# A one-core chain of four transformer layers in fp32: how the kernel passes from one matrix product to the next

## The chip, the cores and the metric

The kernel runs on one core of one Trainium2 chip. Its time is the device time of one execution in microseconds. Before the change it took 2042.35 us, the median of three runs (2042.11 to 2044.91).

## What is computed

A residual stream x of 256 positions by 1024 features passes through two blocks of two layers each.

```python
# first block, l = 0, 1
h = h + mixer_l(rms_norm(h, mix_norm_g[l]))             # l=0: attention || gated linear attention; l=1: RG-LRU
h = h + conv_ffn(rms_norm(h, ffn_norm_g[l]), ...)       # x @ w_up, causal conv, u*gelu(g), @ w_down
x = rms_norm(h, final_norm_g)
# second block, l = 0, 1
x = x + 0.5 * rms_norm(swiglu(rms_norm(x, ffn1_pre[l]), ...), ffn1_post[l])
x = x + rms_norm(hybrid_mixer(rms_norm(x, mix_pre[l]), ...), mix_post[l])
x = x + 0.5 * rms_norm(swiglu(rms_norm(x, ffn2_pre[l]), ...), ffn2_post[l])

def rms_norm(x, g): return x * rsqrt(mean(x * x, -1) + 1e-6) * g
def swiglu(h, w_gate_up, w_down): g, u = split(h @ w_gate_up, 2); return (silu(g) * u) @ w_down
```

The inner widths are 3072 (first block) and 2816 (second). All data are fp32 and all weights are read once.

## The kernel before

**Layout.** Features lie on the 128 partitions and the 256 positions on the free axis, so x is 8 tiles of 128x256. A weight matrix comes from memory as chunks of 16 blocks of 128x128 (1 MB). A chunk usually holds 8 blocks along the inner dimension for each of two output tiles. There are 313 chunks.

**A product in three.** Each fp32 operand is split in two fp32r parts: ScalarE rounds a raw chunk (`w_raw`) to `w_hi` (`round_chunk`, L222), VectorE takes the rest `w_lo` (`rest_chunk`, L230), and in the same way `x_split` (L315 hi, L320 lo) and `h_split` hold the two parts of an activation. TensorE then does three matmuls of 128x128 by 128x256 per block: hi·hi (L246), hi·lo (L248) and lo·hi (L250), 48 for a chunk, into one PSUM bank that holds the chunk's two output tiles.

**Rings.** `w_raw`, `w_hi`, `w_lo` and the PSUM banks are rings of `RING = 3`. When chunk n is multiplied, ScalarE rounds chunk n+3 (`refill_hi`) and VectorE makes the rest of chunk n+2 (`refill_lo`). SyncE fetches raw chunk n once the rest of chunk n-3 is done. TensorE waits before a chunk for its `w_lo` and for `pair_taken`; this starts at 2, so that it runs at most two chunks ahead of VectorE's evictions although there are three banks.

**Order.** Every engine has its instruction stream written out in program order, with semaphores; there is no scheduler. A pass through the program is, in phases: ev_in, attention, ev_out, up0, down0, od_xr, od_gate, od_ax, od_out, up1, down1, then twice upA, downA, bg, pool_in, cv, gates, conv_out, pool, pool_out, w_o, upB, downB. The chunks within a phase mostly stand in register loops of three, and the two layers of the second block are one outer loop on each engine.

**Norms.** `rms_norm` is applied after the product: a phase that begins with a norm (`pre_pe`) multiplies x times the gain, and its results are scaled by 1/rms when they are taken out of PSUM (`take_scaled`, L264). The 1/rms vector is made on the way. Squares are summed on ScalarE and VectorE, TensorE sums over partitions (`mean_pe`, L285, in the middle of the second chunk), ScalarE takes the root (`rms_act`, L291), VectorE the reciprocal and two diagonal matrices (`rinv_dve`, L296, L299), TensorE spreads them to all partitions (`rinv_pe`, L305) and ScalarE copies (`rinv_act`, L311).

**The two kinds of transition.** Where a residual is added at once (ev_out, down0, od_out), `out_dve` adds the product to x (L458) pair by pair and the next phase's splits follow. Where a norm stands after the product (down1, downA, w_o, downB), nothing of the next phase can start before the norm is known: `out_pe`, `out_act`, `out_dve`, then `mean_pe`, `rms_act`, `rinv_dve`, `rinv_pe`, then `post_dve`, `post_act` and `post_pool`, which apply the norm (L377), add it to x (L383 on VectorE for pairs 0 and 2, L399 on GpSimd for pairs 1 and 3), and split x for the next phase. I call this a post transition; there are seven, the last one ends the kernel.

## Time and profile before

| | |
|---|---|
| median of 3 runs | 2042.35 us |
| the profiled execution | 2043.53 us |
| its span, first to last instruction | 2041.7 us |
| TensorE matmul busy | 1899.5 us (93%) |
| VectorE busy | 1372.9 us (67%) |
| ScalarE busy | 942.4 us (46%) |
| granted TensorE clock, mean | 0.96 of full |

The profile gives for each engine when an instruction ran and what ended the idle time before it. Matmuls overlap, so the duration of one (285 ns) is not the time that it adds: the distance between two starts is.

### The profile page before, as it was taken

The page shows a single profiled execution, that of the slowest core. Times are in us where ns is not written, and L with a number is a line of the kernel's source. Part 1 is how long each engine was busy: PE and PEld are TensorE (multiplying, and loading weights), DVE is VectorE, ACT ScalarE, POOL GpSimd, SP SyncE. Part 2 cuts the span into 40 slices and gives each one's busy share as a digit, 9 for nine tenths or more (in the row PEclk, how much of TensorE's full clock was granted, in tenths as well). Part 3 has the DMA queues.
Part 4 walks back from the last instruction along what each step waited for, and adds up shares of the span by engine and source line. Part 5 has one row for each costly group of instructions (what it writes and reads, how often), then busy time and mean ns, then how long its engine had stood idle before and what let it go on. Part 6 is the DMA issues. An engine that isn't in the chain of part 4 may idle for free.

```text
span 2041.7 us, 38654 instructions
## 1 busy us (share of the span) xinstructions
PE 1899.5 (93%) x15258; PEld 1864.6 (91%) x15258; DVE 1372.9 (67%) x1651; ACT 942.4 (46%) x1103; POOL 145.6 (7%) x134
## 2 busy tenths in 40 slices
PE   7969999996999989998999999998999899989996
PEld 7948999996999989997999889998999899989996
DVE  4796898477899456655775666656654686675656
ACT  4443665455666444443354444434443335344444
POOL 0000222000122000000300000000000120000000
PEclk9968999997999989998999999998999899989998
DMA  6312455542455435453444435543554345444453
GB/s 257 131 42 104 169 178 180 183 165 98 171 185 182 179 134 185 179 194 140 168 180 172 169 141 183 188 185 128 182 206 186 124 166 185 166 144 166 184 207 123
DMA packets 46756, 337.27 MB, mean 165 GB/s; under 512 B 5184, under 2 KB 5568, under 8 KB 5952
## 3 DMA queue, kind: packets, MB, share of 16 engines
q1 hardware_dynamic: 46512, 335.34, 45.2%
q8 instruction: 71, 1.16, 0.2%
q0 software_dynamic: 144, 0.52, 0.1%
q14 instruction: 29, 0.24, 0.0%
HBM read 334.80 MB, written 1.05 MB: 164 GB/s over the span
## 4 chain that ended last, share of the span: by engine, by line
PE 60%; issue 29%; DVE 7%; POOL 2%; ACT 2%; DMA 0%; ACTq 0%; POOLq 0%; SPq 0%; DVEq 0%
PE psum L246 19%; PE psum L250 19%; PE psum L248 19%; DVE w_lo L230 1%; POOL scratch L1279 1%; DVE scratch L1126 1%; POOL x_resid L399 0%; DVE scratch L377 0%; DVE x_split L320 0%; POOL scratch L1276 0%; DVE scratch L1372 0%; PE psum L305 0%; DVE scratch L264 0%; DMA params<-par_in 0%; DVE scratch L1096 0%
## 5 line engine op out<-in xcount | busy, mean ns | idle before, releaser
L246 PE MATMUL psum<-x_split,w_hi 128*128 128x256 f32 x3272 | 939.3, 287 | 54.6 <-DVE x_split L320 26.2
L222 ACT ACTIVATE w_hi<-w_raw 128x2048 fp32r<-128x2048 f32 x316 | 604.9, 1915 | 813.8 <-PE psum L250 807.7
L248 PE MATMUL psum<-x_split,w_hi 128*128 128x256 f32 x3272 | 933.2, 285 | 0.0
L250 PE MATMUL psum<-x_split,w_lo 128*128 128x256 f32 x3272 | 933.0, 285 | 0.0
L230 DVE TENSOR_TENSOR w_lo<-w_raw,w_hi 128x2048 fp32r<-128x2048 f32 x315 | 722.2, 2294 | 55.8 <-ACT w_hi L222 55.8
L246 PEld LDWEIGHTS psum<-x_split,w_hi 128*128 128x128 f32 x3272 | 635.6, 194 | 66.3 <-issue 46.0
L248 PEld LDWEIGHTS psum<-x_split,w_hi 128*128 128x128 f32 x3272 | 636.0, 194 | 0.1
L250 PEld LDWEIGHTS psum<-x_split,w_lo 128*128 128x128 f32 x3272 | 635.6, 194 | 0.0
L246 PE MATMUL psum<-h_split,w_hi 128*128 128x256 f32 x1664 | 475.4, 286 | 25.8 <-DVE h_split L1252 18.4
L248 PE MATMUL psum<-h_split,w_hi 128*128 128x256 f32 x1664 | 473.4, 284 | 0.0
L250 PE MATMUL psum<-h_split,w_lo 128*128 128x256 f32 x1664 | 473.2, 284 | 0.0
L246 PEld LDWEIGHTS psum<-h_split,w_hi 128*128 128x128 f32 x1664 | 322.0, 193 | 29.0 <-issue 22.7
L264 DVE TENSOR_TENSOR scratch<-psum,inv_rms 128x512 f32<-128x512 f32 (+1 forms) x205 | 140.8, 689 | 306.3 <-PE psum L250 278.5
L248 PEld LDWEIGHTS psum<-h_split,w_hi 128*128 128x128 f32 x1664 | 322.2, 194 | 0.0
L250 PEld LDWEIGHTS psum<-h_split,w_lo 128*128 128x128 f32 x1664 | 322.0, 194 | 0.0
L560 DVE SCALAR_TENSOR_TENSOR scratch<-scratch,params 128x255 f32<-128x255 f32 x192 | 123.2, 702 | 8.1 <-ACT scratch L506 8.0
L399 POOL TENSOR_TENSOR x_resid<-x_resid,scratch 128x512 f32<-128x512 f32 x12 | 17.4, 1450 | 1228.3 <-DVE scratch L377 1228.3
L460 DVE COPY scratch<-psum 128x512 f32<-128x512 f32 x24 | 16.6, 692 | 111.8 <-PE psum L250 111.8
L498 ACT ACTIVATE h_split<-scratch 128x256 f32 (+1 forms) x136 | 55.1, 405 | 20.2 <-POOL scratch L608 12.7
L614 POOL TENSOR_TENSOR h_split<-scratch,h_split 128x256 f32 (+1 forms) x48 | 44.4, 926 | 165.9 <-ACT h_split L498 165.9
L458 DVE TENSOR_TENSOR x_resid<-psum,x_resid 128x512 f32<-128x512 f32 x16 | 11.1, 692 | 66.8 <-PE psum L250 66.8
L492 ACT ACTIVATE scratch<-scratch 128x256 f32<-128x256 f32 x136 | 54.8, 403 | 0.3
(178 smaller groups left out, 944.9 us busy)
## 6 DMA issues: line engine op xcount, KB each, us to landing
w_raw<-stream_in SPq DMA_DIRECT2D x316, 1024.0 KB, 4.8
x_resid<-x_in SPq DMA_DIRECT2D x1, 1024.0 KB, 6.9
y_out<-x_resid SPq DMA_DIRECT2D x1, 1024.0 KB, 3.9
scratch<-mask_in SPq DMA_DIRECT2D x1, 768.0 KB, 12.8
scratch<-ev_in SPq DMA_DIRECT2D x1, 512.0 KB, 11.4
scratch<-inv_in POOLq DMA_DIRECT2D x1, 512.0 KB, 4.0
params<-par_in SPq DMA_DIRECT2D x1, 247.0 KB, 7.1
matrices<-mat_in SPq DMA_DIRECT2D x1, 192.0 KB, 8.8
```

What stands on the lines that cost most here:

```text
L222: act.activation(w_hi[:, slot, :], raw[:, slot, :], ACT.Copy).then_inc(hi_ready, 1)
L230: dve.tensor_tensor(w_lo[:, slot, :], raw[:, slot, :], w_hi[:, slot, :].bitcast(F32), ALU.subtract).then_inc(lo_ready, 1)
L246: pe.matmul(dst, w_hi[:, c.slot, b:b + P], src[:, k0 + k, 0, :], start=first and k == 0 and m == 0, stop=False)
L248: pe.matmul(dst, w_hi[:, c.slot, b:b + P], src[:, k0 + k, 1, :], start=False, stop=False)
L250: done = pe.matmul(dst, w_lo[:, c.slot, b:b + P], src[:, k0 + k, 0, :], start=False, stop=last and k == nk - 1 and m == tiles - 1)
L264: dve.tensor_tensor(dst, bank(c.slot, tiles), rinv[:, :].unsqueeze(1).to_broadcast([P, tiles, T]), ALU.mult).then_inc(pair_taken, 1)
L492: act.activation(S1(GEL + s), S1((ACC + 2 * s + 1) if conv else (PRE + 2 * s)), func)\
L498: act.activation(hs[:, bass.ds(c.n - prev, 1), 0, :], S(HID + s), ACT.Copy)\
L560: dve.scalar_tensor_tensor(out=scr[:, ACC + 2 * s + t, d:T], in0=scr[:, PRE + 2 * s + t, 0:T - d], scalar=conv[0][:, bass.ds(((c.n - prev) ...
L614: pool.tensor_tensor(hs[:, bass.ds(c.n - prev, 1), 1, :], S(HID + s), hs[:, bass.ds(c.n - prev, 1), 0, :].bitcast(F32), ALU.subtract)\
L1126: ins = dve.tensor_tensor(qd(t)[o:o + 32, h * P:(h + 1) * P].rearrange("p (m n) -> p m n", n=n), E[o:o + 32, :, 1, :], Q[o:o + 32, :, 1, : ...
L1279: pool.tensor_tensor(S(DIFF, 2), S(DIFF, 2), pair, ALU.subtract).then_inc(*pool_diff.one())
```

## The change

- **Rings.** `RING` is 4 for `w_hi` and `w_lo`, `w_raw` keeps 3 buffers (`RAWS`). PSUM has `BANKS = 4` for chunk pairs, and `pair_taken` starts at 4. ScalarE now rounds chunk n+4 after chunk n, VectorE makes the rest of n+3.
- **First two chunks together.** `alternating` runs the first two chunks of a norm phase, and of the phases with one chunk for each output pair (ev_out, od_out, conv_out, pool_out, w_o), side by side in two banks: first all that needs the hi part of the activation, tile by tile, then all that needs the lo part.
- **Last tile apart.** In the last group of an output phase, the last chunk is multiplied output tile by output tile (`tile_by_tile`), tile 7 in a bank of its own (`SPLIT`), so that tile 6 is taken out while tile 7 is multiplied.
- **Sum of squares.** At a post transition TensorE sums the squares of tiles 0 to 5, 6 and 7 in three steps; the squares of tile 7 are read from PSUM. In a norm phase the mean stands in the third chunk after its fourth of eight steps, and the spreading after its seventh.
- **1/rms.** The diagonal matrices are gone: TensorE multiplies the reciprocal, broadcast as the stationary matrix, by the identity (two 128x128 matmuls for one of 128x256).
- **`post_dve`** does all residual additions on VectorE (GpSimd does none), in the groups 0, 1, 2-3, 4-5, 6-7, and all lo splits after them. The refills for the last chunk go behind it.
- **Straight code.** All register loops but SyncE's are written out, the outer loop too; the per-layer copy of the parameters goes. Three padding chunks are no longer fetched and split.
- **End and start.** The result leaves in four transfers, each after its pair of tiles; the last post transition makes no splits. At the start raw chunk 2 is fetched after the constants, and the spreading for ev_in comes as before after chunk 1.

The diff, cut to its core (`self.bank`, `self.buf` and renamed calls are left out):

```diff
-RING = 3
+RING = 4
+RAWS = 3
+BANKS = 4
+SPLIT, AXBANKS = 5, (4, 5, 7)
...
         def refill_lo(dve, c):
-            rest_chunk(dve, (c.slot + 2) % RING, c.number + 2)
+            rest_chunk(dve, c.number + RING - 1)
...
+        def alternating(pe, first, second, src, nk, hi, lo, k0=0):
+            both = (first, second)
+            for c in both:
+                pe.wait_ge(pair_taken, c.event + 1)
+                pe.wait_ge(lo_ready, c.number + 1)
+            for k in range(nk):
+                pe.wait_ge(*hi(k0 + k))
+                for c in both:
+                    for m in range(2):
+                        b = (k * 2 + m) * P
+                        for w in (w_hi, w_lo):
+                            pe.matmul(tile(c.bank, m), w[:, c.slot, b:b + P], src[:, k0 + k, 0, :],
+                                      start=k == 0 and m == 0 and w is w_hi, stop=False)
+            for k in range(nk):
+                pe.wait_ge(*lo(k0 + k))
+                for c in both:
+                    for m in range(2):
+                        b = (k * 2 + m) * P
+                        done = pe.matmul(tile(c.bank, m), w_hi[:, c.slot, b:b + P], src[:, k0 + k, 1, :],
+                                         start=False, stop=k == nk - 1 and m == 1)
+                    if k == nk - 1:
+                        done.then_inc(chunk_done, 1)
...
-                ins = dve.tensor_scalar(diag[:, h, :], IDENT, small[:, 4 + h:5 + h], float(D),
-                                        ALU.mult, ALU.mult)
+                ins = pe.matmul(RINV[:, h * P:(h + 1) * P], small[:, 4 + h:5 + h].to_broadcast([P, P]), IDENT,
+                                start=h == 0, stop=h == 1)
...
+        def tile_by_tile(pe, c, both, src, k0, nk, first, ready, tr, post, l):
+            for m, dst in enumerate(both):
+                for k in range(nk):
+                    ...
+                    if post is not None and m == 1 and k == nk // 2:
+                        pe.wait_ge(*tr["acc"].count(2, l))
+                        sums_pe(pe, (sqacc[:, 0, :], sqacc[:, 1, :]), True, False)
+                done.then_inc(*(tr["tile6_done"].one() if m == 0 else (chunk_done, 1)))
+            if post is not None:
+                pe.wait_ge(*tr["sq6"].count(1, l))
+                sums_pe(pe, (sqb[:, 0, :],), False, False)
+                pe.wait_ge(*tr["sq7"].count(1, l))
+                sums_pe(pe, (sqb[:, 1, :],), False, True).then_inc(*post["stat"].one())
+                rinv_pe(pe, post, l)
...
+            for ks in ((0,), (1,), (2, 3), (4, 5), (6, 7)):
+                k, n = ks[0], len(ks)
+                for j in ks:
                     h = x[:, j, :] if final else S1(HB + j)
                     dve.scalar_tensor_tensor(out=h, in0=h, scalar=gain[:, j:j + 1], in1=RINV, ...)
+                if not final:
+                    dve.wait_ge(*tr["y"].count(k + n, l))
+                    dve.tensor_tensor(x[:, k:k + n, :], x[:, k:k + n, :], S(HB + k, n), ALU.add)
+            for k in range(KT):
+                split_lo(dve, nxt, ngain, k, next_layer)
...
+            refill_lo(dve, last)
...
-            for c in chunks(act, phase, n, l, peel=3):
-                at = c.n if isinstance(c.n, int) else n
+            for c in chunks(phase, n, l):
+                at = c.n
                 act.wait_ge(chunk_done, c.number + 1)
-                if at == 1:
-                    rinv_act(act, pre, l)
                 refill_hi(act, c)
                 if at == 0:
                     chunk0 = c
+                    continue
+                if at == 1:
                     rms_act(act, pre, l)
-                    continue
+                    rinv_act(act, pre, l)
...
+            for g in range(4):
+                sp.wait_ge(*post_x(PN["postB"], 2 * g + 1, LAYERS2 - 1, False))
+                sp.dma_start(out[:, 2 * g:2 * g + 2, :], x[:, 2 * g:2 * g + 2, :]).then_inc(out_landed, 16)
```

On VectorE, from the end of downA to the take-out of bg's first chunks, the program had these rows before (registers left out; L460 takes out the last pair, L472 adds its squares, L230 is a weight chunk's rest):

```order
L460 COPY scratch<-psum 128x512 [waits chunk_multiplied]
...
L472 TENSOR_TENSOR square_sum<-square_sum,squares 128x512 [waits downA_squared]
...
L230 TENSOR_TENSOR w_lo<-w_raw,w_hi 128x2048 [waits chunk_hi_ready]
...
L296 RECIPROCAL small<-small 128x2 [waits postA_stat]
...
L299 TENSOR_SCALAR inv_rms_diagonal<-matrices,small 128x128 [waits postA_stat]
L299 TENSOR_SCALAR inv_rms_diagonal<-matrices,small 128x128
...
L377 SCALAR_TENSOR_TENSOR scratch<-scratch,params_layer,psum 128x256 [waits postA_stat]
```

and has these now, down to the same take-out (L512 tiles 6 and 7, L394 the norm, L399 the residual, L338 the lo splits, L219 a weight chunk's rest, L280 the take-out):

```order
L512 COPY scratch<-psum 128x256 [waits downA_tile6_done]
L512 COPY scratch<-psum 128x256 [waits downA_sq7,chunk_multiplied]
L316 RECIPROCAL small<-small 128x2 [waits postA_stat]
L394 SCALAR_TENSOR_TENSOR scratch<-scratch,params,psum 128x256 [waits postA_stat]
L399 TENSOR_TENSOR x_resid<-x_resid,scratch 128x256 [waits postA_y_ready]
...
L338 SCALAR_TENSOR_TENSOR x_split<-x_resid,params,x_split 128x256 [waits normM_hi_ready] x8
L410 TENSOR_TENSOR square_sum<-scratch 128x512 [waits postA_squared]
L410 TENSOR_TENSOR square_sum<-square_sum,scratch 128x512 [waits postA_summed,postA_squared] x2
L219 TENSOR_TENSOR w_lo<-w_raw,w_hi 128x2048 [waits chunk_hi_ready] x3
L316 RECIPROCAL small<-small 128x2 [waits normM_stat]
L280 TENSOR_TENSOR scratch<-psum,inv_rms 128x512 [waits chunk_multiplied,normM_stat]
```

The weight rest and the diagonals are gone from between the squares and the norm; three rests stand together ahead of the next phase's reciprocal. On ScalarE the same stretch now reads (L495, L502 squares of tiles 6 and 7, L311 the root, L333 the hi splits, L210 a weight chunk rounded, L329 the copy of 1/rms):

```order
L495 ACTIVATE squares<-scratch 128x256 [waits downA_tile6_taken]
L502 ACTIVATE squares<-psum 128x256 [waits chunk_multiplied]
L311 ACTIVATE small<-psum,small 128x2 [waits postA_stat]
L333 ACTIVATE x_split<-x_resid,params 128x256 [waits postA_x_ready] x8
L382 ACTIVATE scratch<-x_resid 128x512 x4
L210 ACTIVATE w_hi<-w_raw 128x2048 [waits chunk_landed_2]
L210 ACTIVATE w_hi<-w_raw 128x2048 [waits chunk_landed_0,chunk_multiplied]
L210 ACTIVATE w_hi<-w_raw 128x2048 [waits chunk_landed_1,chunk_multiplied]
L311 ACTIVATE small<-psum,small 128x2 [waits normM_stat]
L329 ACTIVATE inv_rms<-psum 128x256 [waits normM_stat]
```

where before the root of the next norm stood behind two rounded chunks of that stretch (one after the last chunk, one after bg's first), and now behind three.

## Rows read from the trace of the kernel before

**Rows 1.** The page: span, and busy time of two engines.

```profile
span 2041.7 us, 38654 instructions
PE 1899.5 (93%) x15258; PEld 1864.6 (91%) x15258; DVE 1372.9 (67%) x1651; ACT 942.4 (46%) x1103; POOL 145.6 (7%) x134
```

**Rows 2.** Stretches: length, busy and (matmuls) by engine, granted clock, DMA share, GB/s.

```profile
30.00:50.00 20.00, 20.00 (x169) 20.00 (x168) 8.67 (x6) 5.75 (x3) 0.00 (x0) 1.00 0.49 172
230.00:330.00 100.00, 100.00 (x836) 100.00 (x835) 96.16 (x108) 60.37 (x86) 28.55 (x36) 1.00 0.52 186
940.00:945.00 5.00, 4.75 (x22) 4.45 (x21) 4.97 (x10) 1.81 (x4) 1.56 (x2) 0.50 0.01 3
1010.00:1100.00 90.00, 90.00 (x752) 90.00 (x751) 60.38 (x70) 42.24 (x48) 0.00 (x0) 1.00 0.50 181
```

**Rows 3.** Timeline of the post transition from downA to bg, by engine.

```profile
930.09 0.28 PE L250 MATMUL psum<-h_split,w_lo 128*128 128x256 f32 x1
930.40 0.69 DVE L460 COPY scratch<-psum 128x512 f32<-128x512 f32 x1 [5.84 <-PE psum L250]
931.13 0.63 ACT L443 ACTIVATE squares<-scratch 128x512 f32<-128x512 f32 x1 [3.04 <-DVE scratch L460]
932.40 2.29 DVE L230 TENSOR_TENSOR w_lo<-w_raw,w_hi 128x2048 fp32r<-128x2048 f32 x1
932.54 1.05 PE L285 MATMUL psum<-matrices,square_sum 128*128 128x1 f32 x8 [2.17 <-DVE square_sum L472]
933.63 0.26 ACT L291 ACTIVATE small<-psum,small 128x2 f32<-128x2 f32 x1 [1.87 <-PE psum L285]
934.60 0.16 DVE L296 RECIPROCAL small<-small 128x2 f32<-128x2 f32 x1
935.33 1.22 PE L305 MATMUL psum<-inv_rms_diagonal,matrices 128*128 128x256 f32 x2 [1.74 <-DVE inv_rms_diagonal L299]
936.59 0.87 DVE L377 SCALAR_TENSOR_TENSOR scratch<-scratch,params_layer,psum 128x256 f32<-128x256 f32 x2 [1.31 <-PE psum L305]
937.49 0.69 DVE L383 TENSOR_TENSOR x_resid<-x_resid,scratch 128x512 f32<-128x512 f32 x1
938.22 0.91 ACT L315 ACTIVATE x_split<-x_resid,params_layer 128x256 fp32r<-128x256 f32 x2 [2.53 <-DVE x_resid L383]
939.51 0.55 PE L246 MATMUL psum<-x_split,w_hi 128*128 128x256 f32 x1 [2.96 <-DVE x_split L320]
956.88 0.35 PE L246 MATMUL psum<-x_split,w_hi 128*128 128x256 f32 x1 [1.44 <-DVE scratch L264]
```

**Rows 4.** Other waits of TensorE in the timeline.

```profile
173.53 0.38 PE L246 MATMUL psum<-h_split,w_hi 128*128 128x256 f32 x1 [1.49 <-DVE h_split L1184]
431.76 0.36 PE L246 MATMUL psum<-x_split,w_hi 128*128 128x256 f32 x1 [1.77 <-issue]
493.00 0.58 PE L246 MATMUL psum<-h_split,w_hi 128*128 128x256 f32 x1 [1.40 <-DVE h_split L1252]
1006.28 0.38 PE L246 MATMUL psum<-x_split,w_hi 128*128 128x256 f32 x1 [3.07 <-DVE w_lo L230]
1115.68 0.38 PE L246 MATMUL psum<-h_split,w_hi 128*128 128x256 f32 x1 [1.09 <-DVE scratch L1372]
1384.58 0.58 PE L246 MATMUL psum<-x_split,w_hi 128*128 128x256 f32 x1 [5.39 <-issue]
```

**Rows 5.** The page: a weight chunk rounded and fetched.

```profile
L222 ACT ACTIVATE w_hi<-w_raw 128x2048 fp32r<-128x2048 f32 x316 | 604.9, 1915 | 813.8 <-PE psum L250 807.7
w_raw<-stream_in SPq DMA_DIRECT2D x316, 1024.0 KB, 4.8
```

**Rows 6.** Timeline at the end of the kernel, and the result's transfer.

```profile
2028.39 0.87 DVE L377 SCALAR_TENSOR_TENSOR scratch<-scratch,params_layer,psum 128x256 f32<-128x256 f32 x2 [1.31 <-PE psum L305]
2035.73 1.44 POOL L399 TENSOR_TENSOR x_resid<-x_resid,scratch 128x512 f32<-128x512 f32 x1 [3.44 <-DVE scratch L377]
2037.25 0.35 SPq L1420 DMA_DIRECT2D y_out<-x_resid  x1
```

More of the change, by code:

```diff
@@ L242, in multiply @@
                     pe.wait_ge(*ready(k0 + k))
[L243 removed]
+                for m, dst in enumerate(tiles_):
                     b = (blk0 + k * 2 + m) * P
[L245 to L251 removed]
@@ L252, in multiply @@
-                if midway is not None and k == nk // 2 - 1:
-                    midway()
+                    opens = first and k == 0 and (m == 0 or dst is not tiles_[0] and first == "apart")
+                    pe.matmul(dst, w_hi[:, c.slot, b:b + P], src[:, k0 + k, 0, :], start=opens, stop=False)
+                    pe.matmul(dst, w_hi[:, c.slot, b:b + P], src[:, k0 + k, 1, :], start=False, stop=False)
+                    done = pe.matmul(dst, w_lo[:, c.slot, b:b + P], src[:, k0 + k, 0, :], start=False,
+                                     stop=last and k == nk - 1 and m == len(tiles_) - 1)
@@ L423, in out_pe @@
+        def out_pe(pe, phase, per, src, nk, hi, lo, l, k0=0, tr=None, post=None):
+            if per == 1:
+                alternating(pe, Chunk(phase, 0, l), Chunk(phase, 1, l), src, nk, hi, lo, k0)
+            for g, cs, pair, event in groups(phase, per, l):
+                if per == 1 and g < 2:
+                    continue
                 pe.wait_ge(pair_taken, event + 1)
+                apart = tr is not None and g == 3
+                both = [tile(pair, 0), tile(SPLIT, 0)] if apart else pair_tiles(pair)
@@ L452, in out_dve, with sum_squares @@
+            def sum_squares(g):
+                if g > 1:
+                    dve.wait_ge(*tr["acc"].count(g - 1, l))
+                dve.wait_ge(*tr["sq"].count(g + 1, l))
+                dve.tensor_tensor(sqacc[:, :, :], sqacc[:, :, :], sqb[:, :, :], ALU.add)\
+                   .then_inc(*tr["acc"].one())
+            for g, cs, pair, event in groups(phase, per, l):
                 for c in cs[:-1]:
@@ L1287, in hybrid_dve @@
             for g in G4:
[L1288 removed]
+                c = Chunk("bg", g, l)
                 if g == 0:
```

579 lines of the change are left out of this document (289 added, 290 removed).

## The prediction

> **What bounds the kernel now.** I read the page's busy times first: TensorE is busy 93% of 2041.7 us, VectorE 67% [rows 1]. Then the stretches, for TensorE's pace: 752 matmuls in 90 us and 836 in 100 us, both at full clock, are 0.120 us each [rows 2]. At the half level (granted clock 0.50) 22 take 4.75 us, 0.216 each [rows 2]. The weights give 48 matmuls a chunk, 24 for ev_in's last chunk and 36 for the last chunk of each output pair in downA and downB, in all 14,808. At 0.120 us they need 1777 us. The change leaves them as they are, so only the other 265 us can move. Some 85 of these lie in ev_in and the attention, a chain between engines that the change hardly touches.
>
> The timeline shows where the rest lies. At a post transition TensorE starts its last matmul at 930.09 and the next phase's first at 939.51; then it runs slowly for some us and stops again before the third chunk, which starts at 956.88 [rows 3]. That chunk takes 5.76 us, so from last matmul to the end of chunk 2 (I count a phase's chunks from 0) it is 32.55 us, for 144 matmuls worth 17.3. Six transitions look like this; the kernel's end is the seventh. Other waits stand in rows 4.
>
> **A post transition, up to the norm.** Call R the end of the spreading matmuls. Before, R is 6.5 us after the last matmul's start (930.09 to 936.59) [rows 3]. In it lie the take-out of both tiles (0.69), squares (0.63) and sum, eight mean rows (1.05), root (0.26), a reciprocal that stood behind a weight rest (root ends 933.89, reciprocal starts at 934.60), diagonals, and the spreading (1.22) [rows 3]. Now: 0.31 to matmul end and wake-up; squares of one tile from PSUM, 0.40 by half of a pair's split (0.91) less overlap; 0.06; half of the mean's rows, 0.55; 0.03 and root 0.26; 0.03 and reciprocal 0.16; 0.06; spreading 1.1. The last has as many columns, in four pieces: bounds 0.6 (at full clock, an estimate as half of 1.22) and 1.5; I take 1.1 since the clock may already be low. Sum 2.95. The sum over tiles 0 to 5 now stands in the stream of tile 7 and costs TensorE about 0.95. The squares of tile 6 are hidden behind tile 7 (18 or 24 matmuls, 2.2 or 2.9 us). So R comes 2.6 us sooner.
>
> **From R to the end of chunk 2.** Before: 936.55 to 962.64, 26.1 us [rows 3]. Now, in us after R:
> - VectorE: a norm takes 0.43, an addition 0.42 or 0.69, so x is ready at 0.9 and 1.7, then by pairs at 3.2, 4.7, 6.3. Eight lo splits at 0.40 (taken as fast as the norms of [rows 3]) end at 9.5, three sums of 0.7 at 11.6, the rest of weight chunk 2 (2.29) at 13.9.
> - TensorE: tile 0's hi part is there at 1.4. 96 matmuls need 11.5; it waits 0.4 for tile 2; the clock is low for 4 to 5 us of it, which costs 2.0. In [rows 2] it was low after the 9.4 us gap; the new gap is 4.4 with a little work inside, and I take the same level but a shorter stretch. Both chunks are done at 15.0.
> - SyncE may fetch raw chunk 5 only when the rest of chunk 2 is done: 13.9, plus 4.8 to land [rows 5], 18.7. ScalarE rounds it (1.9 [rows 5]) ahead of the root, because the order puts three rounded chunks there. The root ends at 20.9, the reciprocal at 21.1.
> - TensorE reaches the spreading at 15.0 + 0.95 (mean) + 42 x 0.12 = 21.0. The two paths meet. Spreading 0.65 and six matmuls end chunk 2 at 22.5.
> - No wait ahead of chunk 3: four banks, and its take-outs are two chunks away.
>
> A transition becomes 0.95 + 2.95 + 22.5 = 26.4 us against 32.55, a gain of 6.15. With residual there are five, 30.8 us. The final norm has no addition but must take tile 7 out before squaring it: 5.5. The turn of the outer loop showed 5.39 idle where the others show 2.96 [rows 4, 3]; part of it came back in what followed, I add 1.7. Sum **38.0**.
>
> **The other phases.**
> - cv waited 3.07 us for a weight rest held up by the pool windows on VectorE [rows 4], and the clock fell after it. The rest of cv's chunk 2 is now made one take-out earlier. 3.2 + 1.4 for the low clock, two layers: **9.2**. VectorE's load is unchanged; if its lag only moves, this is 0.
> - pool and the start of pool_out waited four times like [rows 4] at 1115.68, 3.8 us in all, for banks. With four banks the pool steps run through, but pool_out's pair starts behind VectorE's second step (6.1 us after conv_out); 3.4 less, 0.9 of it lost ahead of w_o, whose first two chunks need two rests at once. Two layers: **5.0**.
> - ev_in, up0 and up1 had the stop ahead of a third chunk as at 956.88, which four banks take away: 1.1, 1.5, 1.7, **4.3**. VectorE then takes out up0's first chunk 5 us later than before. It is busy 96% there [rows 2], so the lag stays for most of the phase; with three rests ahead and four banks I find 2.9 us of room.
> - ev_out: the 1.49 us wait for the lo part [rows 4] goes, since 32 matmuls need only the first hi parts: **1.8**.
> - od_xr and od_gate: the stop ahead of chunk 2 and the 1.77 us wait with its low clock [rows 4] go, but VectorE, with the convolution between take-out and rest longer a chunk than TensorE, makes TensorE wait about 0.9 us three times: **2.1**.
> - od_out: TensorE starts 16 matmuls on the first two hi parts and is fed until the last arrives at 493.0, where it stood still before [rows 4]. Done 2.2 us sooner at low clock, 5.1 at full: **4.0**.
> - The end: R is 2.6 sooner. From R x was complete after 8.8 (2028.39 to 2037.17) and the span ended at 13.3 [rows 6]; now x is complete after 6.3 and the last quarter needs about 3, between 2 and the 4.45 that the whole took [rows 6]: **6.6**.
> - Loops written out: stretches with loops (230 to 330) and without (30 to 50) have the same pace, 0.120 and 0.118 [rows 2]. **0**.
>
> Sum 71 us: span 1970.7, execution 1972.5. The shown median is 1.2 below the profiled 2043.53, so **1971**.
>
> [...]
>
> **Rivals.**
> - A, as summed: 1971, its own range 1963 to 1981. For it: each term removes a wait that a row shows. Chance 0.50.
> - B, the weight pipeline takes the place: three raw buffers feed four, and three rests and three roundings stand in a row. If the fetch of chunk 5 or the rests come 3 us later, that is 3 x 6 = 18 us, and if cv or od keep their waits, more: 1990. For it: the two paths to the spreading meet within 0.1 us. Against it: VectorE idles later in these phases. Chance 0.20.
> - C, the clock does not fall, or recovers sooner, in the shorter gaps: 1 us at od_out, the spreading at 0.6, the mean cheaper: 1962. It is little, because the path over chunk 5 holds chunk 2 anyway. Chance 0.17.
> - D, the inner loops cost a bit everywhere: 836 matmuls at 0.1183 leave 1.1 us in nearly six turns, 0.2 a turn; 58 turns on TensorE make 12 us: 1959. [...] Against it: one matmul more or less in the 20 us stretch is half of that difference. Chance 0.05.
> - E, slower: TensorE's program grows from 5,621 to 14,386 rows, and code that runs once must be fetched while 1 MB chunks come in. To eat 71 us the 8,765 added rows must cost 8.1 ns each, 7% of the pace. Against it: the straight stretch in ev_in ran at full pace with DMA half busy (0.49) [rows 2]. At 10 ns each: 2059. Chance 0.05.
> - F, the change hardly moves the time, since each wait only wanders to the next engine: 2041. Nothing shows a second engine above 67% over the span. Chance 0.03.
>
> **How the numbers follow.** B, C and D bound the range: 1960 to 1990 leaves out E, F and the outer parts of B and D. About 0.2% (4 us) can be told from no change. Faster: A to D, 0.92. Same: 0.03. Slower: 0.05.
>
> **What would show it.** The first matmul of a norm phase 4.4 us after the last one; the third chunk's end 26.4 us after it; no wait of TensorE at cv's third chunk; TensorE's wait ahead of the spreading under 0.5 us, and ScalarE waiting for the landing of a raw chunk there. If ScalarE waits for w_raw for 3 us or more ahead of the root, B holds. If matmuls in the middle of up0 stand further apart than 0.120, E holds.

## The result, and the profile after

The changed kernel takes 1972.7 us (median of 4 runs, 1972.55 to 1975.29), the kernel before on the same chip 2043.26 us (4 runs, 2042.11 to 2044.91). The ratio is 0.965, with a 95% interval of 0.9637 to 0.9662: 71 us faster. The prediction was 1971, with a range from 1960 to 1990.

The page of the profiled execution, span and busy times, answers to [rows 1]:

```profile
span 1970.9 us, 35690 instructions
PE 1889.2 (96%) x15348; PEld 1864.9 (95%) x15348; DVE 1342.4 (68%) x1623; ACT 932.7 (47%) x1095; POOL 139.4 (7%) x122
```

TensorE's busy time fell by 10.3 us (1899.5 to 1889.2), the span by 70.8: some 60 us of what went was idle time. The stretches answer to [rows 2] (length, busy and matmuls by engine, granted clock, DMA share, GB/s):

```profile
30.00:50.00 20.00, 20.00 (x166) 19.89 (x165) 10.01 (x9) 8.14 (x5) 0.00 (x0) 1.00 0.64 228
220.00:320.00 100.00, 100.00 (x836) 100.00 (x835) 97.22 (x109) 65.00 (x91) 36.94 (x38) 1.00 0.54 189
916.60:921.00 4.40, 4.33 (x25) 4.36 (x26) 4.30 (x10) 2.33 (x5) 0.00 (x0) 0.64 0.00 0
1010.00:1080.00 70.00, 70.00 (x586) 70.00 (x585) 40.84 (x40) 32.60 (x34) 0.00 (x0) 1.00 0.52 180
```

In the middle of up0 100 us again hold 836 matmuls, now in straight code, and 586 in 70 us is the same 0.120 us each. The stretch from 1010 to 1080 us had no stop.

The transition from downA to bg in the timeline answers to [rows 3] (rows of weight matmuls, and repeats, are left out). L512 takes out tiles 6 and 7, L495 and L502 square them, L300 are rows of the mean, L322 the spreading, L394 the norm, L399 the residual, L333 the hi splits, L338 the lo splits:

```profile
910.89 0.95 PE L300 MATMUL psum<-matrices,square_sum 128*128 128x1 f32 x8
912.38 0.28 PE L455 MATMUL psum<-h_split,w_lo 128*128 128x256 f32 x1
912.50 1.24 PE L300 MATMUL psum<-matrices,squares 128*128 128x1 f32 x8
912.70 0.38 ACT L502 ACTIVATE squares<-psum 128x256 f32<-128x256 f32 x1 [2.17 <-PE psum L455]
913.78 0.26 ACT L311 ACTIVATE small<-psum,small 128x2 f32<-128x2 f32 x1 [0.70 <-PE psum L300]
914.08 0.17 DVE L316 RECIPROCAL small<-small 128x2 f32<-128x2 f32 x1 [0.47 <-ACT small L311]
914.30 0.71 PE L322 MATMUL psum<-matrices,small 128*128 128x128 f32 x4 [0.55 <-DVE small L316]
915.56 0.42 DVE L399 TENSOR_TENSOR x_resid<-x_resid,scratch 128x256 f32<-128x256 f32 x1
916.67 0.55 PE L261 MATMUL psum<-x_split,w_hi 128*128 128x256 f32 x1 [1.67 <-ACT x_split L333]
...
926.65 4.49 DVE L219 TENSOR_TENSOR w_lo<-w_raw,w_hi 128x2048 fp32r<-128x2048 f32 x2
929.11 5.24 SPq L1489 DMA_DIRECT2D w_raw<-stream_in  x3
932.51 0.95 PE L300 MATMUL psum<-matrices,square_sum 128*128 128x1 f32 x8
933.98 1.91 ACT L210 ACTIVATE w_hi<-w_raw 128x2048 fp32r<-128x2048 f32 x1 [2.46 <-DMA w_raw<-stream_in]
935.80 0.24 ACT L311 ACTIVATE small<-psum,small 128x2 f32<-128x2 f32 x1
936.08 0.17 DVE L316 RECIPROCAL small<-small 128x2 f32<-128x2 f32 x1 [2.23 <-ACT small L311]
936.29 0.71 PE L322 MATMUL psum<-matrices,small 128*128 128x128 f32 x4 [0.57 <-DVE small L316]
```

The spreading ends at 915.01, 2.63 us after the last matmul's start (before 6.5), and TensorE starts again at 916.67. The second half shows the path over a raw chunk, as the prediction drew it: the first of the two rests ends at about 928.9 (it is the rest of chunk 2), SyncE issues the fetch at 929.11, ScalarE rounds it from 933.98, and only then come the root and the reciprocal. The two paths do meet: TensorE stands 0.57 us ahead of the spreading. There is no stop ahead of the fourth chunk.

What TensorE waits for now (in total, times, longest):

```profile
PE psum L261 <- ACT h_split L1000: 16.3, 3, 15.4
PE psum L237 <- DVE x_split L338: 10.3, 1, 10.3
PE psum L261 <- ACT x_split L333: 9.5, 6, 1.7
PE psum L859 <- DVE scratch L1196: 9.0, 9, 1.5
PE psum L322 <- DVE small L316: 5.3, 10, 0.6
...
PE psum L237 <- DVE w_lo L219: 2.2, 3, 1.0
```

The first row is the wait between od_ax and od_out, where the chain of ScalarE and VectorE is the same as before; the second and fourth lie in ev_in and the attention. What is left of the six transitions is 1.2 us (once) or 1.7 us (five times) ahead of the first matmul. Ahead of a spreading TensorE waits ten times: 0.55 us at each of the seven post norms, and 0.57, 0.26 and 0.58 us in three norm phases.

### The profile page after: what moved, and what is told of

The parts are those of the page before. It is cut to its first block, busy times and chain, and to the rows that moved or that the text cites. A ratio compares the mean times of both kernels' runs of the same rounds, so it can differ in the third digit from the quotient of the medians.

```text
span 1970.9 us, 35690 instructions
## 1 busy us (share of the span) xinstructions
PE 1889.2 (96%) x15348; PEld 1864.9 (95%) x15348; DVE 1342.4 (68%) x1623; ACT 932.7 (47%) x1095; POOL 139.4 (7%) x122
## 3 DMA queue, kind: packets, MB, share of 16 engines
q8 instruction: 121, 1.98, 0.4%
## 4 chain that ended last, share of the span: by engine, by line
PE 86%; DVE 9%; ACT 2%; DMA 2%; issue 1%; SPq 0%; DVEq 0%; ACTq 0%
PE psum L237 24%; PE psum L238 24%; PE psum L239 24%; PE psum L261 6%; PE psum L268 3%; DVE w_lo L219 2%; DMA w_raw<-stream_in 1%; PE psum L300 1%; PE psum L452 1%; DVE scratch L1196 1%; PE psum L455 1%; PE psum L454 1%; DVE scratch L394 1%; DVE x_resid L399 1%; PE psum L322 1%
## 5 line engine op out<-in xcount | busy, mean ns | idle before, releaser
L210 ACT ACTIVATE w_hi<-w_raw 128x2048 fp32r<-128x2048 f32 x313 | 598.0, 1913 | 771.1 <-PE psum L239 604.7
L237 PE MATMUL psum<-x_split,w_hi 128*128 128x256 f32 x2984 | 849.9, 285 | 12.5 <-DVE x_split L338 10.3
L238 PE MATMUL psum<-x_split,w_hi 128*128 128x256 f32 x2984 | 846.7, 284 | 0.0
L219 DVE TENSOR_TENSOR w_lo<-w_raw,w_hi 128x2048 fp32r<-128x2048 f32 x313 | 717.5, 2296 | 78.6 <-ACT w_hi L210 78.6
L237 PEld LDWEIGHTS psum<-x_split,w_hi 128*128 128x128 f32 x2984 | 574.5, 193 | 14.3 <-issue 13.2
L238 PEld LDWEIGHTS psum<-x_split,w_hi 128*128 128x128 f32 x2984 | 574.5, 193 | 0.1
L239 PEld LDWEIGHTS psum<-x_split,w_lo 128*128 128x128 f32 x2984 | 574.4, 192 | 0.0
L237 PE MATMUL psum<-h_split,w_hi 128*128 128x256 f32 x1264 | 358.3, 283 | 2.1 <-ACT scratch L984 2.1
L238 PE MATMUL psum<-h_split,w_hi 128*128 128x256 f32 x1264 | 358.3, 283 | 0.0
L239 PE MATMUL psum<-h_split,w_lo 128*128 128x256 f32 x1264 | 358.2, 283 | 0.0
L280 DVE TENSOR_TENSOR scratch<-psum,inv_rms 128x512 f32<-128x512 f32 (+1 forms) x205 | 139.6, 688 | 255.4 <-PE psum L239 239.2
L237 PEld LDWEIGHTS psum<-h_split,w_hi 128*128 128x128 f32 x1264 | 243.0, 192 | 2.3 <-ACT scratch L984 2.3
L238 PEld LDWEIGHTS psum<-h_split,w_hi 128*128 128x128 f32 x1264 | 243.0, 192 | 0.0
L239 PEld LDWEIGHTS psum<-h_split,w_lo 128*128 128x128 f32 x1264 | 243.0, 192 | 0.0
L512 DVE COPY scratch<-psum 128x512 f32<-128x512 f32 (+1 forms) x30 | 17.5, 584 | 121.6 <-PE psum L239 70.1
L261 PE MATMUL psum<-x_split,w_hi 128*128 128x256 f32 x288 | 80.1, 312 | 9.5 <-ACT x_split L333 9.5
L261 PE MATMUL psum<-h_split,w_hi 128*128 128x256 f32 x256 | 65.3, 294 | 18.3 <-ACT h_split L1000 16.3
L1348 POOL TENSOR_TENSOR scratch<-scratch 128x512 f32<-128x512 f32 x8 | 10.3, 1292 | 916.3 <-DVE scratch L1385 916.3
L261 PEld LDWEIGHTS psum<-x_split,w_hi 128*128 128x128 f32 x288 | 63.2, 219 | 10.7 <-issue 10.7
```

The lines of the kernel that those rows point to most:

```text
L210: act.activation(w_hi[:, n % RING, :], raw[:, n % RAWS, :], ACT.Copy).then_inc(hi_ready, 1)
L219: dve.tensor_tensor(w_lo[:, n % RING, :], raw[:, n % RAWS, :], w_hi[:, n % RING, :].bitcast(F32), ALU.subtract).then_inc(lo_ready, 1)
L237: pe.matmul(dst, w_hi[:, c.slot, b:b + P], src[:, k0 + k, 0, :], start=opens, stop=False)
L238: pe.matmul(dst, w_hi[:, c.slot, b:b + P], src[:, k0 + k, 1, :], start=False, stop=False)
L239: done = pe.matmul(dst, w_lo[:, c.slot, b:b + P], src[:, k0 + k, 0, :], start=False, stop=last and k == nk - 1 and m == len(tiles_) - 1)
L261: pe.matmul(tile(c.bank, m), w[:, c.slot, b:b + P], src[:, k0 + k, 0, :], start=k == 0 and m == 0 and w is w_hi, stop=False)
```

## Where the 71 us came from

I measured for each phase the starts of its matmuls, and took off 0.120 us for each. A transition here goes from the last matmul's start to the end of chunk 2, as in the prediction. The shorter wait ahead of od_out's first matmul (15.4 instead of 16.5 us) is counted with od_ax, the wait ahead of w_o's with pool_out.

| term | predicted | measured |
|---|---|---|
| six post transitions, net of the mean in the stream | 38.0 | 39.0 |
| cv's third chunk, two layers | 9.2 | 9.5 |
| pool, pool_out, less the loss ahead of w_o | 5.0 | 3.6 |
| ev_in, up0, up1 | 4.3 | 4.7 |
| ev_out | 1.8 | 1.7 |
| od_xr and od_gate | 2.1 | 2.3 |
| od_ax | 0 | -0.6 |
| od_out | 4.0 | 3.9 |
| the end | 6.6 | 6.8 |
| sum | 71.0 | 70.9 |

The six distances were 31.75, 32.61, 32.61, 34.31, 32.49 and 32.73 us (sum 196.5) and are 24.28, 25.17, 25.67, 25.15, 25.48 and 26.43 (152.2); from the difference of 44.3 go off 0.89 us for the mean's rows in the stream, six times. The terms sum to the whole difference of the two profiled executions. Each is one execution of each kernel; what the clock alone moves in such a term is told at the end.

## The experiments

Each ratio is against the kernel before, timed on the same chip. One per mille is 2 us.

**e1: the first two chunks one after the other.**

```diff
-            for k in range(nk):
-                pe.wait_ge(*hi(k0 + k))
-                for c in both:
+            for c in both:
+                for k in range(nk):
+                    pe.wait_ge(*hi(k0 + k))
+                    pe.wait_ge(*lo(k0 + k))
...
-                        for w in (w_hi, w_lo):
+                        for w, part in ((w_hi, 0), (w_hi, 1), (w_lo, 0)):
```

> The changed kernel, with the first two chunks of a phase multiplied one after the other instead of side by side. Theory of the prediction: in a post transition the lo splits start only when all of x is ready, 6.3 us after the spreading, so the first chunk starts there (6.7) and not at 1.4, and chunk 2 ends near 27.5 instead of 22.5 after it: 5 us at six places, 4 at od_out, 3 at each pool_out, 1.7 at ev_out, in all about 42 us, 2014 us. Rival: the low clock after a gap and the path over the fetch of raw chunk 5 hold chunk 2 anyway, so that side by side is worth at most 1 us a place, under 10 us in all.

Measured: 2015.85 us, ratio 0.9861 (0.9845 to 0.9878), 43 us slower than the changed kernel. The theory holds. This order is the largest single part of the change, because VectorE's lo splits now stand behind all residuals, and without it TensorE must wait for them:

```profile
925.94 1.22 PE L316 MATMUL psum<-matrices,small 128*128 128x128 f32 x4 [0.55 <-DVE small L310]
...
933.44 1.27 DVE L332 SCALAR_TENSOR_TENSOR x_split<-x_resid,params,x_split 128x256 fp32r<-128x256 f32 x3
933.55 0.91 ACT L327 ACTIVATE x_split<-x_resid,params 128x256 fp32r<-128x256 f32 x2 [0.60 <-DVE x_resid L393]
934.06 0.55 PE L262 MATMUL psum<-x_split,w_hi 128*128 128x256 f32 x1 [6.90 <-ACT x_split L327]
```

The idle time is put down to ScalarE, whose split of tile 0 (at 928.18) was long done; what ends it is the first lo split, on VectorE from 933.44. In the profiles the six transitions sum to 180.8 us instead of 152.2, pool_out loses 3.9 us in each layer (w_o gives 0.5 back), od_out 2.9 and ev_out 1.8: some 40 us. The other 3.5 us by which e1's profiled execution is longer lie ahead of ev_out's first matmul, in ev_in and the attention (159.5 instead of 155.9 us), where the edit changes nothing. So the order is worth some 40 of the 71 us.

**e2: the root ahead of a rounded chunk.**

```diff
+                if at == 1:
+                    rms_act(act, pre, l)
                 refill_hi(act, c)
...
                 if at == 1:
-                    rms_act(act, pre, l)
                     rinv_act(act, pre, l)
```

> The changed kernel, with the root of a norm phase ahead of the rounding of the weight chunk for which ScalarE waits until it has landed. Theory: TensorE's own path and the path over the landing nearly meet, so the root is late by 0.4 to 0.7 us at three of the ten norm phases and in time at the others: 1 to 2 us faster, 1971. Rival (the weight pipeline has taken the place of the old waits): ScalarE waits 64 us in all for raw chunks, 32 times, and taking the root out from behind gives 3 us at each of six places, 18 us faster, 1955.

Measured: 1970.9 us, ratio 0.9642 (0.9626 to 0.9658), which can't be told from the changed kernel's 0.965. The waits ahead of a late spreading are gone (seven of TensorE's L322 waits are left, all at a post norm), and the six distances sum to 151.5 instead of 152.2. So the path over the raw chunk is real but almost as long as TensorE's own: freeing it took away three waits of 1.4 us in all, and what is left of that in the sum is 0.7 us, less than the clock moves in a single transition (last section).

**e3: tiles 6 and 7 multiplied together in the last chunk.**

```diff
-            for m, dst in enumerate(both):
-                for k in range(nk):
-                    pe.wait_ge(*ready(k0 + k))
+            for k in range(nk):
+                pe.wait_ge(*ready(k0 + k))
+                for m, dst in enumerate(both):
```

> The changed kernel, with the last chunk's two tiles (in their two banks) multiplied step by step together again, so that tile 6 is done only 3 matmuls before tile 7. Theory: the take-out and squares of tile 6 then stand ahead of the squares of tile 7 on ScalarE, 0.5 us later at seven places, 3.5 us slower, 1976. Rival: the tile order carries most of the 2.6 us by which the norm came sooner, 1.5 to 2 us a place, 10 to 14 us slower.

Measured: 1978.06 us, ratio 0.9684 (0.967 to 0.970), 5 us slower by the medians and 7 by the ratios. That is nearer to the theory's 3.5 than to the rival's 10 to 14, and above it. The squares of tile 6 are no longer hidden behind tile 7, and the mean waits for squares at each of the seven transitions, 4.1 us in all (in the changed kernel at one, 0.6). This is the theory's part. What it left out is w_o, where the sum over tiles 0 to 5 is late too (1.65 and 1.59 us instead of 0.55 and 0.46):

```profile
1134.24 1.05 PE L300 MATMUL psum<-matrices,square_sum 128*128 128x1 f32 x8 [1.65 <-DVE square_sum L519]
1139.35 1.05 PE L300 MATMUL psum<-matrices,squares 128*128 128x1 f32 x8 [0.33 <-ACT squares L496]
```

**e4: the refill for the last chunk ahead of tile 6's take-out.**

```diff
-            refill_lo(dve, last)
...
+                if nxt is None:
+                    refill_lo(dve, c)
                 dve.wait_ge(*tr["tile6_done"].count(1, l))
```

> The changed kernel, with the rest of the weight chunk that stood behind a post transition moved ahead of tile 6's take-out, into 3.7 us in which VectorE is idle. Raw chunk 5 of the next phase is then fetched some 17 us sooner. Theory: the same three late spreadings as in the run with the root first go, 1 to 2 us faster, 1971. Rival: the rest ahead delays the take-out of tile 6 and with it the norm by 2 us at the three short downA and downB chunks each, 4 to 8 us slower.

Measured: 1974.95 us (1970.64 to 1975.44), ratio 0.9664 (0.9648 to 0.9681): no gain that shows. The timing can't rule out the low end of the rival's loss (4 us). The profiled execution is the fastest of the four (1970.64, the others 1974.9 to 1975.44); its distances sum to 152.0 instead of 152.2. The three late spreadings are gone, as expected. New is a wait at w_o, twice: the rest (2.29 us) holds up tile 6's take-out, and the mean waits 0.8 us for its squares.

**e5: three chunks ahead instead of four.**

```diff
-            return pair_taken, event + BANKS + 1
+            return pair_taken, event + 4
...
-            pe.sem_inc(pair_taken, BANKS)
+            pe.sem_inc(pair_taken, 3)
```

> The changed kernel, but pair_taken starts at 3, so TensorE runs at most three chunks ahead of the evictions although four banks are there. Everything else, the four weight buffers too, stays. Theory of the prediction: cv's stop went because the rest is made one take-out earlier, so it stays gone; but the fourth chunk of each of the nine norm phases must wait for the first take-out, about 0.8 us, and the pool steps wait for banks again (2.3 us a layer): 7 + 5 = 12 us slower than the changed kernel, ratio 0.971, about 1984 us. Rival: the banks, not the rests, removed cv's stop. Then cv also waits again (4.7 us a layer), 21 us slower, ratio 0.976, about 1994.

Measured: 1985.31 us, ratio 0.9711 (0.9698 to 0.9724). The theory holds, the rival falls: cv needs 46.08 us, exactly 384 x 0.120, so its stop did not go with the banks. What is left is the earlier rest, which the fourth weight buffer allows; no run takes that buffer away alone. The new stop ahead of the fourth chunk:

```profile
941.01 1.88 DVE L280 TENSOR_TENSOR scratch<-psum,inv_rms 128x512 f32<-128x512 f32 x3 [1.22 <-ACT inv_rms L329]
941.75 0.39 PE L237 MATMUL psum<-x_split,w_hi 128*128 128x256 f32 x1 [0.49 <-DVE scratch L280]
```

In up0 the fourth chunk (chunk 3) now starts 19.37 us after the last matmul of ev_out instead of 18.72, and through its end each of the nine norm phases has lost 0.75 us there. The pool steps themselves run through; the wait for a bank stands behind them, ahead of pool_out, and is 2.3 us longer a layer, the size expected for the steps. pool_out then loses 1.3 and 2.7 us more, which I had not counted. The fourth bank is worth 12 to 13 us.

**e6: the diagonal matrices back.**

```diff
+            for h in range(2):
+                ins = dve.tensor_scalar(diag[:, h, :], IDENT, small[:, 4 + h:5 + h], float(D), ...)
...
-                ins = pe.matmul(RINV[:, h * P:(h + 1) * P], small[:, 4 + h:5 + h].to_broadcast([P, P]), IDENT, ...)
+            ins = pe.matmul(RINV, ONES, diag[:, :, :].rearrange("p h t -> p (h t)"), start=True, stop=True)
```

> The changed kernel, but 1/rms is spread as before: VectorE makes two diagonal matrices of the reciprocal, TensorE multiplies ones by them in two 128x256 matmuls. Theory: the diagonals cost 0.55 us at a post transition, and the spreading 1.22 instead of 0.71, since the few matmuls on 256 columns run at the low clock; 7 x 1.1 = 7.5 us, and 0.2 us in each of nine norm phases: 9 us slower than the changed kernel, ratio 0.970, about 1982. Rival: what TensorE does costs the same in both forms and only VectorE's 0.55 us count: 4 us, ratio 0.9675, about 1977.

Measured: 1980.39 us, ratio 0.9692 (0.9678 to 0.9705). It lies at the theory's end, 0.970; the rival's 0.9675 is just outside the interval. The transition's rows:

```profile
913.61 0.17 DVE L317 RECIPROCAL small<-small 128x2 f32<-128x2 f32 x1 [0.47 <-ACT small L312]
913.81 0.48 DVE L320 TENSOR_SCALAR inv_rms_diagonal<-matrices,small 128x128 f32<-128x128 f32 x2
914.35 1.22 PE L327 MATMUL psum<-inv_rms_diagonal,matrices 128*128 128x256 f32 x2 [1.07 <-DVE inv_rms_diagonal L320]
```

In the changed kernel the spreading took 0.71 at a granted clock of 1.00 (914.30 to 915.10) and 1.22 at 0.50 (1138.30 to 1139.60). The old form does the same in e6: at another transition, where the clock was 1.00, it took 0.70 (length, busy by engine, clock):

```profile
1540.14:1540.84 0.70, 0.69 (x2) 0.29 (x2) 0.00 (x0) 0.00 (x0) 0.00 (x0) 1.00 0.00 0
```

So the form of the matmuls doesn't set their time, the clock does, and the expectation had the size right but gave the number of columns as part of the reason, wrongly. That the clock fell here because TensorE stood idle 0.5 us longer isn't shown: in e2 the spreading at downA takes 1.23 us after an idle time of 0.55.

**e7: the rest behind the take-out of tile 7, ahead of the reciprocal.**

```diff
-            refill_lo(dve, last)
...
-                    refill_lo(dve, c)
+                refill_lo(dve, c)
```

> The changed kernel, but VectorE makes the rest of a weight chunk right after it took out the last tile, ahead of the reciprocal, as before the change. Theory: the take-out ends at 1.2 us after the last matmul, the rest (2.29) ends 1.8 us after the reciprocal could have started: six transitions x 1.8 = 11 us slower, less about 1 us because the rest of chunk 2 is done sooner: ratio 0.970, about 1983. Rival: the end of chunk 2 hangs on the path over raw chunk 5 (rest, fetch, rounding, root), which now starts sooner, so the lost time is given back there: no change, 0.965, about 1973.

Measured: 1983.5 us, ratio 0.9706 (0.9693 to 0.9719); the six distances sum to 162.6 us, 10.5 more. The theory holds, and nothing is given back over the raw chunk:

```profile
914.96 2.28 DVE L219 TENSOR_TENSOR w_lo<-w_raw,w_hi 128x2048 fp32r<-128x2048 f32 x1
915.22 0.26 ACT L311 ACTIVATE small<-psum,small 128x2 f32<-128x2 f32 x1 [0.70 <-PE psum L300]
917.16 0.16 DVE L316 RECIPROCAL small<-small 128x2 f32<-128x2 f32 x1
917.37 1.22 PE L322 MATMUL psum<-matrices,small 128*128 128x128 f32 x4 [2.19 <-DVE small L316]
```

The root is done at 915.48, the reciprocal starts at 917.16, behind the rest.

**e8: the kernel before, inner loops written out.**

```diff
-    turns = (count - peel) // RING
-    if turns > 1:
-        with eng.Fori(0, turns) as i:
-            for j in range(RING):
-                yield Chunk(phase, peel + j, i, layer)
-        peel += turns * RING
```

> The kernel before with all inner register loops written out on every engine but SyncE, and only that; the outer loop of the two layers stays. Theory: an inner loop's turn costs nothing that the pace shows: ratio 1.000, 2044 us. Rival D of the prediction: each turn costs 0.2 us on TensorE, about 58 turns: 12 us faster, ratio 0.994. Rival E: straight code costs fetching: slower, at 2 ns a row some 10 to 20 us.

Measured: 2043.59 us, ratio 0.9999 (0.999 to 1.0008). Both rivals fall. From 250 to 320 us, inside up0, it has 586 matmuls, as the kernel before with its loops has:

```profile
250.00:320.00 70.00, 70.00 (x586) 70.00 (x585) 67.28 (x73) 43.05 (x62) 19.40 (x24) 1.00 0.51 182
```

**e12: the kernel before, only the outer loop written out.** The diff shows TensorE's; the loops of ScalarE, VectorE and GpSimd are changed in the same way.

```diff
-            with pe.Fori(0, LAYERS2) as l:
+            for l in range(LAYERS2):
```

> The kernel before with the outer loop of the two layers written out on all engines, inner loops kept. Theory: the turn of the outer loop holds the transition from downB to upA for 1.7 us more than the others (34.31 against 32.6 us from last matmul to the end of chunk 2), and that goes: the distance becomes 32.6, the time about 2 us less, ratio 0.999, which the timing alone hardly tells. Rival: the extra comes from copying the layer's parameters, which this kernel keeps: the distance stays 34.3.

Measured: 2042.01 us, ratio 0.9984 (0.9975 to 0.9993). By the medians it is 2.8 us faster (2044.82 before), by the spans 1.7. At the turn, first matmul of the second upA:

```profile
1374.93 1.63 PE L285 MATMUL psum<-matrices,square_sum 128*128 128x1 f32 x8 [2.24 <-DVE square_sum L472]
1377.72 1.22 PE L305 MATMUL psum<-inv_rms_diagonal,matrices 128*128 128x256 f32 x2 [1.17 <-DVE inv_rms_diagonal L299]
1381.91 0.55 PE L246 MATMUL psum<-x_split,w_hi 128*128 128x256 f32 x1 [2.96 <-DVE x_split L320]
```

The wait before that matmul is 2.96 us as elsewhere [rows 3], instead of 5.39 of "issue" [rows 4], and the distance is 32.54 us instead of 34.31. The kernel before fetches instructions in that place: in the view of its DMA queues from 1376 to 1386 us stands

```profile
q8 instruction: 2, 0.03, 1.1%
```

(packets, MB, share; q8 is a queue that fetches instructions), and e12 has no packet of that queue from 1374 to 1384 us. The copy of the layer's parameters is still there, so it had no part in it.

**e9: the result in one transfer.**

```diff
-            for g in range(4):
-                sp.wait_ge(*post_x(PN["postB"], 2 * g + 1, LAYERS2 - 1, False))
-                sp.dma_start(out[:, 2 * g:2 * g + 2, :], x[:, 2 * g:2 * g + 2, :]).then_inc(out_landed, 16)
+            sp.wait_ge(*post_x(PN["postB"], 7, LAYERS2 - 1, False))
+            sp.dma_start(out, x[:, :, :]).then_inc(out_landed, 16)
```

> The changed kernel, but the result leaves in one transfer of 1 MB after the last tile, as before. Theory: the last quarter (256 KB) lands 2.5 us after its issue, the whole took 4.45 before; 2.0 us slower, ratio 0.9665, and the profile's end moves from 12.2 to about 14.2 us after the last matmul's start. Rival: the quarters ahead of it are still under way and hold the last one back, so that the order of the transfers gives nothing: no change in that distance.

Measured: 1972.67 us, ratio 0.9649 (0.9636 to 0.9662). The time shows no difference. The profile does: the last matmul starts at 1957.32 and the span ends at 1970.86, 13.5 us later, against 12.2 (1958.67 to 1970.89) with four transfers. So the four give 1.3 us, not 2.0. In this profiled execution ev_in and the attention happened to be 1.2 us shorter (154.7 instead of 155.9 us; they take 154.2 to 155.9 in ten of the changed kernel's profiled relatives, and 159.5 in e1), which hides it.

**e10 and e11: e2 and e4 together, and then a folded sum.** e10 has both edits shown above. e11 adds, on VectorE, the halves of the square sum, so that TensorE needs four rows for a mean instead of eight:

```diff
+        def fold(dve, tr, n, l):
+            dve.wait_ge(*tr["acc"].count(n, l))
+            dve.tensor_tensor(sqacc[:, 0, :], sqacc[:, 0, :], sqacc[:, 1, :], ALU.add).then_inc(*tr["acc"].one())
...
-                        sums_pe(pe, (sqacc[:, 0, :], sqacc[:, 1, :]), True, False)
+                        sums_pe(pe, (sqacc[:, 0, :],), True, False)
```

> Two earlier edits together on the changed kernel: the refill for the last weight chunk stands ahead of the last take-out (e4), and the root of a norm phase stands ahead of the rounding of the chunk (e2). Theory: each frees the same path to the spreading of a norm phase, so together they give no more than one of them, 2 us: 1971. Rival: they add up, 1969.

> e10 and one edit more: at the post transitions and in the six norm phases behind them VectorE adds the two halves of the square sum (128x256, 0.42 us), so that TensorE sums one tile instead of two: four rows of the mean instead of eight. Theory: the eight rows stand in TensorE's stream and cost it 0.95 us each time, four cost about half; 13 x 0.45 = 6 us less than e10: 1964 to 1965, ratio 0.962. Rival: the rows in a norm phase are hidden, since the spreading waits for the reciprocal anyway: 7 x 0.45 = 3 us. Rival on the other side: VectorE's extra additions come late and TensorE waits for the sum: no gain.

Measured: e10 1971.91 us, ratio 0.9647 (0.9633 to 0.966); e11 1971.78 us, ratio 0.964 (0.9627 to 0.9653). e10 is as fast as the changed kernel. Neither edit alone showed a gain beyond its interval, and with 2043.26 us before, 1971 and 1969 are ratios of 0.9646 and 0.9637, both within e10's interval, so the timing can't tell the theory from its rival; the six distances sum to 151.8 us, against 151.5 in e2 and 152.0 in e4, and show no sum. e11 missed its 6 us. The six distances even grew, from 151.8 to 153.2 us; the seven output phases got shorter by 0.45 us each. At w_o:

```profile
1134.49 0.42 DVE L389 TENSOR_TENSOR square_sum<-square_sum 128x256 f32<-128x256 f32 x1
1134.83 2.29 DVE L219 TENSOR_TENSOR w_lo<-w_raw,w_hi 128x2048 fp32r<-128x2048 f32 x1
1134.97 0.61 PE L300 MATMUL psum<-matrices,square_sum 128*128 128x1 f32 x4 [0.97 <-DVE square_sum L389]
1137.03 0.42 DVE L517 COPY scratch<-psum 128x256 f32<-128x256 f32 x1
...
1137.95 1.87 PE L300 MATMUL psum<-matrices,squares 128*128 128x1 f32 x8 [1.21 <-ACT squares L500]
```

TensorE first waits 0.97 us for the folded sum, and then again 1.21, since the rest that e4 put there holds tile 6's take-out until 1137.03. With a shorter stream ahead of it TensorE comes to that place sooner and waits longer; the clock is low there (a mean of 0.56 from 1136.60 to 1143.20; the mean's eight rows take 1.87 us; in the changed kernel at downA they take 1.24). This is the rival on the other side. The fold without e4's edit wasn't tried. None of the versions is faster than the changed kernel by more than the intervals tell.

## Why the prediction was right, point by point

- **The bound and the pace** held: the 14,808 matmuls of the weights stand 0.120 us apart, and 71 of the 265 us beside them went.
- **Up to the norm**: 2.95 us were predicted from the last matmul's start to the end of the spreading, 2.63 were measured at downA, since the spreading ran at full clock and took 0.71 instead of 1.1. At w_o the clock was at the low level, and it took 1.22. My two bounds for this row, 0.6 and 1.5, hold both.
- **From there to the end of chunk 2**: predicted 22.5, measured 22.5 (915.01 to 937.55, at downA). Each station is where the prediction had it: rest of chunk 2 done at 13.9 (13.9), both first chunks at 15.0 (14.6), root at 20.9 (21.0). e7 confirms the price of the rest ahead of the reciprocal (10.5 us of six transitions), e1 that of the new order of the first two chunks.
- **The meeting of two paths**: predicted within 0.1 us; TensorE waits for the reciprocal in three of the nine norm phases, 1.4 us in all, and e2 took these waits away. Rival B was right that ScalarE waits for raw chunks more (64.0 us in 32 waits, before 6.1 in 2), but ahead of the root it waited 2.46 us, under the 3 us set as B's sign, and on TensorE's path this shows only by those tenths and perhaps at od_ax.
- **cv**: predicted 9.2, measured 9.5. Of the two reasons, the banks and the rest that comes one take-out earlier, e5 leaves the second, which the prediction gave.
- **pool and w_o**: the net is 3.6 instead of 5.0. Two steps are mis-sized. The bank waits gave 2.95 us a layer where I took 3.4. The loss ahead of w_o for two rests at once is there, 0.6 us where I took 0.9. And one step was missing: in w_o TensorE waits 0.55 us (in the second layer 0.46) in the middle of tile 7 for the sum over tiles 0 to 5, which lies nearer to its squares there than in the longer phases. It costs 0.6 us a layer. The two waits in the first layer:

```profile
1111.74 0.36 PE L261 MATMUL psum<-h_split,w_hi 128*128 128x256 f32 x1 [0.42 <-DVE w_lo L219]
1134.48 0.27 PE L300 MATMUL psum<-matrices,square_sum 128*128 128x1 f32 x1 [0.55 <-DVE square_sum L518]
```

- **od**: three waits of TensorE were predicted at about 0.9 us; there are three of 1.01, 0.58 and 0.56. od_ax loses 0.6, not foreseen: behind a rounding that waits 2.54 us for a raw chunk, ScalarE delivers its part later. I put this down to four rounded chunks on three raw buffers, but didn't try a fourth one.
- **Loops**: 0 was predicted for the inner ones, e8 measured 0.9999 (0.999 to 1.0008). Rival D is out. At the one turn of the outer loop TensorE lost 1.8 us, which e12 gives back; my 1.7 for that turn was the right size. The two kinds of loop also differ in what they fetch: from 212 to 330 us, in up0's loop, the kernel before fetches no packet on instruction queue q8 (e8, with the loop written out, 7), and around the turn of the outer loop it fetches two. The Trainium skill (Runtime: NRT & Kernel Launch, section Instruction fetch mechanics) says that a taken branch stalls the engine when its target isn't in the short window of code that the engine holds, since that code must be fetched first. The trace agrees on both sides: no fetch and no lost time at the short loops, fetches and 1.8 us at the long one. That the fetches make the stall is read from their place, and no run shows it apart.
- **Straight code**: rival E is out. The page counts 121 packets of instruction fetches against 71 before, 1.98 MB against 1.16, and the pace is the same. The 14,386 rows that the rival gives TensorE's new program can't be all of it, since it holds each of the 14,808 weight matmuls once; the trace has 15,348 matmuls. Rival E falls all the same.
- **The end**: 6.6 predicted, 6.8 measured; of these the four transfers are 1.3 (e9). The rest I put down to the earlier norm and to the additions on VectorE alone (x is complete 6.4 us after R, before 8.8); no run takes these two apart.

That the sum came out at 70.9 against 71.0 is in part luck, two errors that cancel: the six transitions gave 1.0 us more than I took, the pool steps 1.4 us less. The first is the clock's, as far as can be seen: the transition from down1 took 24.3 us in the changed kernel, where the clock was at 0.70 in its first 5 us, and 25.5 in e4 and e5, where it was at 0.50 and the edit does nothing to that stretch or, in e4, should shorten it.

## What to carry to other kernels

Find the engine that sets the pace, count its work at its own pace, and look for the gain only in what is left over; then follow one stop of each kind to the engine that is late, station by station. Where an operand arrives in two parts, order the consumer's work so that all that needs the early part comes first, over more than one chunk if there are banks for it: here, over two chunks, that alone was some 40 of 71 us. Once two paths meet within a microsecond, freeing one of them gives only the tenths between them, and a piece of work that is moved out of one wait must be followed to the shortest phase, where it can hold up the next one.

## What the runs showed of the hardware

- **The clock at a transition.** The same four matmuls of the spreading took 0.71 us or 1.22 us. The stretches around them show the granted clock (length, busy by engine, clock):

```profile
1138.30:1139.60 1.30, 1.22 (x4) 0.93 (x4) 0.00 (x0) 0.00 (x0) 0.00 (x0) 0.50 0.00 0
914.30:915.10 0.80, 0.71 (x4) 0.52 (x4) 0.05 (x1) 0.00 (x0) 0.00 (x0) 1.00 0.00 0
```

  At the 2.4 GHz level it is the one, at 1.2 GHz the other. Which it is at a site changes from kernel to kernel, but it seems not to be random, as far as one profiled execution of each can tell: e9, equal to the changed kernel up to the end, repeats its six gaps from last to first matmul, 4.32, 4.28, 4.80, 4.29, 4.29 and 5.18 us against 4.32, 4.29, 4.80, 4.29, 4.29 and 5.21. In e2 and e4, where only ScalarE's or VectorE's order differs, other sites are slow (at downA 4.80 and 4.68 instead of 4.29). So edits worth under a microsecond a site can be hidden by where the clock falls; one whole transition moved by 1.2 us with it (24.3 against 25.5 us, above).
- **The shorter gap didn't spare the low clock.** Behind downA the first matmuls still ran at a mean clock of 0.64 (0.50 before). Over the six phases that follow a post norm, the starts that stood 0.125 to 0.45 us apart cost 12.2 us beyond 0.120 each, against 13.7 before; that is 2.0 a transition, what the prediction took.
